# The delta laps' state chain, moved behind products that stand in the lap anyway

## The reference, cut to what matters

```
lower = where(strict, (k * beta) @ k.T * decay, 0)
t_inv = inverse(I + lower)
u = t_inv @ (v * beta)
w = t_inv @ (k * beta * exp(g_cum))
attn = where(causal, q @ k.T * decay, 0)
q_exp = q * exp(g_cum);  k_dec = k * exp(g_last - g_cum)
# per chunk, in order:
v_new = u - w @ state
o     = q_exp @ state + attn @ v_new
state = state * exp(g_last) + k_dec.T @ v_new
```

## Time and profile before

| | |
|---|---|
| median of 3 runs | 1332.1 us |
| the profiled execution | 1331.89 us |
| its span | 1330.6 us |
| PE busy | 1317.8 us (99%) |
| DVE, ACT, POOL busy | 920.7, 719.3, 92.3 us |
| lap of head 2, from its L1602 to the next | 691.67 to 726.83 us of the span |

### The profile page before, as it was taken

The page is one execution under the profiler, slowest core; times in us unless marked ns, Lnnn a source line. Parts: engine busy times, 40 slices in busy tenths (PEclk is TensorE's granted clock), DMA queues, the critical chain, the costliest instruction groups (busy, mean ns, idle before and its releaser), DMA issues.

```text
span 1330.6 us, 23633 instructions
## 1 busy us (share of the span) xinstructions
PE 1317.8 (99%) x9670; PEld 1184.5 (89%) x9670; DVE 920.7 (69%) x1492; ACT 719.3 (54%) x1271; POOL 92.3 (7%) x197
## 2 busy tenths in 40 slices
PE   9999999999999999999999999999999999999998
PEld 8888999999879999999999998878999887889897
DVE  7876887777877977777767777755666654755553
ACT  7555665556666655567555566554334443744442
POOL 1000000000000000011222233200000000000000
PEclk9999999999999999999999999999999999999999
DMA  8443465553434555554233322356544454465440
GB/s 325 159 159 128 162 221 187 190 190 127 152 133 152 207 187 187 188 175 159 96 128 128 127 96 96 128 186 221 192 171 151 156 189 174 164 220 191 177 153 32
DMA packets 33485, 218.37 MB, mean 164 GB/s; under 512 B 4064, under 2 KB 5600, under 8 KB 7904
## 3 DMA queue, kind: packets, MB, share of 16 engines
q1 hardware_dynamic: 30064, 211.83, 44.1%
q10 hardware_dynamic: 3312, 5.02, 1.2%
HBM read 215.78 MB, written 1.05 MB: 163 GB/s over the span
## 4 chain that ended last, share of the span: by engine, by line
PE 93%; DVE 2%; ACT 2%; DMA 2%; issue 1%; SPq 0%; POOL 0%; ACTq 0%; DVEq 0%; POOLq 0%
PE bank L316 28%; PE bank L318 27%; PE bank L317 26%; PE bank L1704 1%; PE bank L1687 1%; DMA sb_conv<-conv 1%; DMA sb_raw<-stream 1%; PE bank L755 1%; PE bank L704 1%; PE bank L776 1%; PE bank L429 1%; ACT sb_w_hi L270 0%; PE bank L2325 0%; PE bank L1602 0%; PE bank L1594 0%
## 5 line engine op out<-in xcount | busy, mean ns | idle before, releaser
L316 PE MATMUL bank<-sb_h_hi,sb_w_hi 128*128 128x256 f32 x1504 | 432.5, 288 | 0.5 <-DVE sb_w_lo L280 0.3
L317 PE MATMUL bank<-sb_h_lo,sb_w_hi 128*128 128x256 f32 x1504 | 419.5, 279 | 0.0
L318 PE MATMUL bank<-sb_h_hi,sb_w_lo 128*128 128x256 f32 x1504 | 419.5, 279 | 0.0
L278 DVE TENSOR_TENSOR sb_w_lo<-sb_raw,sb_w_hi 128x1024 fp32r<-128x1024 f32 x191 | 233.1, 1220 | 113.4 <-ACT sb_w_hi L270 112.6
L316 PEld LDWEIGHTS bank<-sb_h_hi,sb_w_hi 128*128 128x128 f32 x1504 | 282.3, 188 | 8.2 <-issue 4.1
L317 PEld LDWEIGHTS bank<-sb_h_lo,sb_w_hi 128*128 128x128 f32 x1504 | 282.1, 188 | 2.8 <-issue 1.4
L318 PEld LDWEIGHTS bank<-sb_h_hi,sb_w_lo 128*128 128x128 f32 x1504 | 282.5, 188 | 0.0
L270 ACT CAST sb_w_hi<-sb_raw 128x1024 fp32r<-128x1024 f32 x188 | 196.9, 1048 | 99.3 <-PE bank L318 98.5
L280 DVE TENSOR_TENSOR sb_w_lo<-sb_raw,sb_w_hi 128x1024 fp32r<-128x1024 f32 x191 | 233.1, 1221 | 0.0
L271 ACT CAST sb_w_hi<-sb_raw 128x1024 fp32r<-128x1024 f32 x188 | 197.4, 1050 | 0.0
L316 PE MATMUL bank<-sb_w_hi,sb_h_hi 128*128 128x256 f32 (+1 forms) x512 | 161.9, 316 | 2.6 <-DVE sb_h_lo L463 1.4
(11 more groups left out here) (363 smaller groups left out, 1929.0 us busy)
## 6 DMA issues: line engine op xcount, KB each, us to landing
sb_raw<-stream SPq DMA_DIRECT2D x199, 1024.0 KB, 4.8
sb_row<-rows ACTq DMA_DIRECT2D x3, 512.0 KB, 3.7
sb_x<-x SPq DMA_DIRECT2D x2, 512.0 KB, 5.7
sb_raw<-stream SPq DMA_DIRECT2D x2, 512.0 KB, 6.6
sb_norm_b<-norm_b ACTq DMA_DIRECT2D x4, 256.0 KB, 4.4
out<-sb_x SPq DMA_DIRECT2D x4, 256.0 KB, 2.0
sb_retain<-retain ACTq DMA_DIRECT2D x1, 768.0 KB, 4.1
sb_masks<-mask_full ACTq DMA_DIRECT2D x1, 192.0 KB, 7.0
```

What stands on the lines that cost most here:

```text
L278: V.tensor_tensor(w_lo[:, b, 0:HALF], raw[:, r, 0:HALF], w_hi[:, b, 0:HALF].bitcast(F32), ALU.subtract)
L316: T.matmul(out_ap, l_hi, r_hi, start=start, stop=False, **kw)
L317: T.matmul(out_ap, l_hi, r_lo, start=False, stop=False, **kw)
L318: return T.matmul(out_ap, l_lo, r_hi, start=False, stop=stop, **kw)
```

## The change

It moves the chain of the head behind so that its products follow products that stand in the lap anyway, in the laps of heads 1 to 7:
- `first_values_pe` goes directly behind `products_pe`, where 12 products of the stream stood between (6 products 512 wide in head 7's lap);
- `first_state_pe` goes behind a1, `second_values_pe` behind b1, `outputs_pe` behind a2; the stream pieces between the earlier places close up;
- `store_pe` goes from behind b4 to behind a5.

ACT's copies follow: `first_state_act` and `second_values_act` stand behind `level_a_act(hd, 1)`, and `outputs_act` behind `level_a_act(hd, 2)` and a `hi()`. On DVE `query_sides_dve` goes ahead of `level_b_dve(hd, 3)` and `outputs_dve` behind it. On POOL the blocks of levels 3 and 4 are made ahead of `outputs_pool`. `kdec` gets a second buffer, so that the head ahead can write it while the state product of the head behind hasn't read the other. No arithmetic is changed.

```diff
-        kb, kdec, qexp, nwt = (sb(n, [P, P], scope=scope) for n in ("d_kb", "d_kdec", "d_qexp", "d_nwt"))
+        kb, qexp, nwt = (sb(n, [P, P], scope=scope) for n in ("d_kb", "d_qexp", "d_nwt"))
+        kdec = sb("d_kdec", [P, 2, P], scope=scope)
...
-            need(V, state_mm, hd)
-            V.tensor_scalar(kdec[:], ...)
+            need(V, state_mm, hd - 1)
+            V.tensor_scalar(kdec[:, hd % 2, :], ...)
...
 def delta_pe(hd):
                 products_pe(hd)
+                first_values_pe(hd - 1)
...
-            if first:
-                first_values_pe(hd - 1)
             head_unit_pe(u, 0, 2, 4)
-            if first:
-                first_state_pe(hd - 1)
             if more_v:
-                head_unit_pe(u, 0, 4, 6)
+                head_unit_pe(u, 0, 4, 8)
+                level_a_pe(hd, 1)
                 if first:
-                    second_values_pe(hd - 1)
-                head_unit_pe(u, 0, 6, 8)
-                if first:
-                    outputs_pe(hd - 1)
-                level_a_pe(hd, 1)
+                    first_state_pe(hd - 1)
                 u = unit_d(n, 1)
                 T.wait_ge(conv_d[1], n)
                 head_unit_pe(u, 1, 0, 3)
                 level_b_pe(hd, 1)
+                if first:
+                    second_values_pe(hd - 1)
                 head_unit_pe(u, 1, 3, 5)
                 level_a_pe(hd, 2)
+                if first:
+                    outputs_pe(hd - 1)
...
-            head_unit_pe(u, 0, 4, 5)
-            second_values_pe(hd - 1)
-            head_unit_pe(u, 0, 5, 7)
-            outputs_pe(hd - 1)
+            head_unit_pe(u, 0, 4, 7)
             level_a_pe(hd, 1)
+            first_state_pe(hd - 1)
             head_unit_pe(u, 0, 7, 8)
             u = unit_d(n, 1)
             T.wait_ge(conv_d[1], n)
             head_unit_pe(u, 1, 0, 1)
             level_b_pe(hd, 1)
+            second_values_pe(hd - 1)
             head_unit_pe(u, 1, 1, 2)
             level_a_pe(hd, 2)
+            outputs_pe(hd - 1)
...
-            store_pe(hd - 1)
             head_unit_pe(u, 2, 2, 3, tokens)
             level_a_pe(hd, 5)
+            store_pe(hd - 1)
```

More of the change, by code:

```diff
@@ L1761, in key_sides_dve @@
             V.wait_ge(e_last, hd + 1)
-            need(V, state_mm, hd)
-            V.tensor_scalar(kdec[:], bank[6][:, 2 * P:3 * P], small[:, 44:45], None, ALU.mult).then_inc(kdec_done, 1)
+            need(V, state_mm, hd - 1)
+            V.tensor_scalar(kdec[:, hd % 2, :], bank[6][:, 2 * P:3 * P], small[:, 44:45], None, ALU.mult).then_inc(kdec_done, 1)
         def query_sides_dve(hd):
@@ L1791, in first_state_pe @@
             T.wait_ge(kdec_done, hd + 1)
-            T.matmul(b3_[:, 0:A_DV], kdec[:], vn[:, 0, :], start=True, stop=True).then_inc(state_mm, 1)
+            T.matmul(b3_[:, 0:A_DV], kdec[:, hd % 2, :], vn[:, 0, :], start=True, stop=True).then_inc(state_mm, 1)
         def first_state_act(hd):
@@ L2011, in delta_act @@
             hi_half(0)
+            hi_half(1)
+            silu_act(hd, 1)
+            level_a_act(hd, 1)
             if first:
                 first_state_act(hd - 1)
-            hi_half(1)
+            newest_act(n, 0)
             if first:
                 second_values_act(hd - 1)
-            silu_act(hd, 1)
-            level_a_act(hd, 1)
-            newest_act(n, 0)
+            level_a_act(hd, 2)
+            hi()
             if first:
                 outputs_act(hd - 1)
-            level_a_act(hd, 2)
-            hi()
             silu_act(n, 0)
@@ L2073, in delta_dve @@
             vbeta_dve(hd)
-            if first:
-                if more_v:
-                    lo()
-                outputs_dve(hd - 1)
-            level_b_dve(hd, 3)
-            if not first:
+            if first and more_v:
                 lo()
             query_sides_dve(hd)
+            level_b_dve(hd, 3)
+            if first:
+                outputs_dve(hd - 1)
+            else:
+                lo()
             older_dve(n, 1, 1)
@@ L2094, in delta_pool @@
             blocks_pool(hd, 1)
-            blocks_pool(hd, 2)
+            for b in range(2, LEVELS - 2):
+                blocks_pool(hd, b)
             if hd:
                 outputs_pool(hd - 1)
-            for b in range(3, LEVELS - 1):
-                blocks_pool(hd, b)
+            blocks_pool(hd, LEVELS - 2)
         LAST = A_HEADS - 1
@@ L2165, in gate_a_act @@
             hi_half(0)
-            first_state_act(hd - 1)
             hi_half(1)
-            second_values_act(hd - 1)
             silu_act(hd, 1)
             level_a_act(hd, 1)
+            first_state_act(hd - 1)
+            second_values_act(hd - 1)
+            level_a_act(hd, 2)
             outputs_act(hd - 1)
-            level_a_act(hd, 2)
             hi()
@@ L2196, in gate_a_dve @@
             level_b_dve(hd, 1)
+            level_b_dve(hd, 2)
             query_sides_dve(hd)
-            outputs_dve(hd - 1)
-            level_b_dve(hd, 2)
             vbeta_dve(hd)
```

7 lines of the change are left out of this document (3 added, 4 removed).

## The result

The changed kernel takes 1336.87 us (median of 6 executions, 1335.74 to 1337.37), the kernel before 1332.11 (6 executions beside it, 1331.53 to 1332.69). The ratio is 1.0035, 95% interval 1.0024 to 1.0045: 4.8 us slower. The forecast was 1335.9, range 1333.4 to 1338.2.

A forecast was written before the change was run, and what follows sets the result against it. PE, busy 99% of the span, was taken as the bound. Lateness of + 1.5 + 2.0 + 0.4 us less 0.1 for joins gave + 3.8 on 1331.89, 1335.7; 0.2 for the median made 1335.9, range 1333.4 to 1338.2.

The forecast's parts named there:

- three terms of lateness: On PE, a1 or the unit behind it starts late: + 1.5 us heads 1-3, + 2.0 heads 4-6, + 0.4 head 7.
- the joins: First values, first state and second values beside other groups save 0.01 to 0.02 us each; 0.1 us counted in all.
- A: Each of 21 joins on PE saves 0.10 us, 2.1 us less, while the waits stand: 1333.8; chance 0.14.
- B: Joins on PE save 0.14 us each and the waits for kdec and L297 are hidden: 1329.2; chance 0.05.
- D: Waits on kdec and lo are covered and the joins give 0.3 us: 1331.8; chance 0.06.
- C: DVE's outputs delay level 4's subtraction, so a5 waits too in six laps: + 3.0 us more, 1338.9; chance 0.10.
- The estimate of 0.4: Slack of about 0.4 us in the short laps before DVE's outputs, ahead of level 4's subtraction, would make a5 wait.

The follow-up runs named there:

- orders-only kernel: The changed kernel with first state, second values and outputs back at their old places on PE and ACT: 1332.87 us, ratio 1.0003.
- the joined values: The kernel before with only the first values moved directly behind the products: 1332.00 us, ratio 0.9999.
- the values made twice: The changed kernel with the first product of the first values made twice in heads 1 to 7: 1337.17 us, against 1336.87.

## Why the prediction was right, and which terms were off

**The mechanism held, step by step.**
- kdec comes no earlier. It starts 7.73 us behind the lap's first L1603 (692.61 to 700.34), predicted 7.74. The second buffer of kdec bought no earlier start. It is there because the state product of the head behind now stands behind an a1 that waits for the new kdec.
- a1 starts 0.49 us behind kdec's start in the short laps (predicted 0.49). Its lateness there is 0.64, predicted 0.66. In the long laps a1 doesn't wait for kdec at all, where a wait of 0.06 was predicted: in head 2's it starts 0.21 behind the L318 ahead of it, as where nothing holds it, and 0.55 behind kdec's start.
- The unit behind the state product waits for L297 in heads 1, 2, 3 and 7. Lateness 0.54 in head 2's lap (predicted 0.43 to 0.55), and in head 7's, by the same sum from the rows below, 864.99 - (863.68 + 0.38 + 0.44) = 0.49, predicted 0.4.

```profile
863.68 0.45 PE L1688 MATMUL bank<-sb_d_xt,sb_d_low_b 64*64 64x64 f32 x8
...
864.99 0.50 PE L316 MATMUL bank<-sb_w_hi,sb_h_hi 128*128 128x512 f32 x1 [0.23 <-DVE sb_w_lo L297]
```

- Laps grow by 0.54 to 0.64 (long, predicted 0.5), 0.66 to 0.75 (short, 0.66) and 0.52 (head 7, 0.4).
- The three terms of lateness (long laps, short laps, head 7's) come to 3.96 us over the orders-only kernel, predicted 3.9.

**Where two misses cancelled.** The prediction had the L316 start 0.05 us behind the end of L297, from a row of head 0's lap; it starts 0.15 behind it in heads 1 to 3 (and 0.05 in head 7's). And it had a1 of head 2 due 8.17 us into the lap (699.84 - 691.67); it comes at 8.28, of which 0.09 is the slower pace of some 20 products ahead of it. The later start of the unit adds 0.10 us to the lateness and the later a1 takes 0.11 off it. So the path, the waits and their order were right for the reasons given, but that the long laps' size came out to some hundredths is luck.

**The term that was off** is the joins. The prediction gave them - 0.1 us; they cost + 0.43. Standing next to another group does save what was measured: b1 and second values, 704.25 to 705.92 less 0.23, take 1.44 us, and apart they took 0.58 + 0.87 = 1.45. What was left out is that the stream's pace between groups is not one number (last section). Of the 0.97 us between 1335.9 and 1336.87 the laps make 0.59, 0.53 of it by the joins. The 0.6 us outside the laps would be more than the rest, but the medians differ by 4.76 us where the two profiled executions differ by 5.07.

**The rivals.** A (joins pay 0.10 each) is refuted for the first values by the joined values (0.9999), and for a wide product behind a level by the rows: b1 and second values save 0.01, and a2 with the outputs behind it takes 1.88 us (707.10 to 709.21, less 0.23), as much as outputs and a1 in the order of before. B and D (no waits) are refuted by the rows. C, that a5 waits behind DVE's outputs, didn't happen: the outputs end at 717.8 and the level-4 subtraction, at 719.39, waits for PE, not for them. Its 0.76 us of idle time was slack of the long lap:

```profile
719.39 0.29 DVE L1716 TENSOR_TENSOR sb_d_xt<-sb_d_xt,bank 128x128 f32<-128x128 f32 x1 [0.76 <-PE bank L1705]
```

The estimate of 0.4 was for the short laps, and there it is about right. DVE in head 5's:

```profile
817.00 0.88 DVE L1516 SCALAR_TENSOR_TENSOR sb_wide<-bank,sb_conv_a,sb_wide 128x255 f32<-128x255 f32 x2 [0.20 <-ACT sb_wide L1508]
817.99 0.29 DVE L1716 TENSOR_TENSOR sb_d_xt<-sb_d_xt,bank 128x128 f32<-128x128 f32 x1
```

The subtraction starts 0.57 us behind b4's start, as in head 2's, and 0.11 behind the end of the work ahead of it. a5 could follow its end by 0.15, at 818.43, and starts at 818.70. So 0.11 + 0.27 = 0.38 us was left, by an estimate from these rows.

The rival that a slower lap has other roots than a1's place is refuted twice: by the orders alone (no loss) and by the values made twice (3.0 us of work for 0.05).

## What to carry to other kernels

On an engine that never waits, small groups between the products of the stream are not overhead to be gathered: they are also the time in which other engines prepare the next step. Before taking a group from ahead of a step, ask when the other engine's result for that step, and for the one behind it, is ready; if the step stood there just in time, the group's time comes back as a wait. And a wait's price is how late the step starts against its unhindered start, not the idle time in the row, which is smaller by the overlap of pipelined products (0.54 for 0.28, 0.64 for 0.57, and 0.30 for no row at all). Whether a step is held is read from its start against the end of what it needs.
